# Two layers of a hybrid diffusion block: the reordered boundary of the layers, and five weight tiles of layer 1 abreast

## The reference

```python
for l in range(DEPTH):                                   # DEPTH = 2
    mod_l = split(silu(c) @ ada_w[l] + ada_b[l], 6)      # shift, scale, gate for two sub-layers
    mod_c = split(silu(c_ctx) @ ada_w[l] + ada_b[l], 6)
    hl = rmsnorm(xl, norm_mix_pre[l]) * (1 + mod_l[1]) + mod_l[0]
    hc = rmsnorm(xc, norm_mix_pre[l]) * (1 + mod_c[1]) + mod_c[0]
    zl, zc = hl @ w_in[l], hc @ w_in[l]                  # 24 tiles of 128 columns
    ... four branches of token mixing on z (attention, scan), gates from h, output projection w_o
    xl = xl + mod_l[2] * rmsnorm(m_l, norm_mix_post[l])
    f_l = conv_ffn(modulate(rmsnorm(xl, norm_ffn_pre[l]), mod_l[3], mod_l[4]), ...)   # ffn_up, ffn_down
    xl = xl + mod_l[5] * rmsnorm(f_l, norm_ffn_post[l])
    # the context stream goes through the same in layer 0 only
```

## Time and profile before

| | us |
|---|---|
| median of 3 runs | 1652.36 (1651.51 to 1654.15) |
| profiled execution | 1652.26 |
| its span | 1650.2 |
| TensorE busy (matmuls) | 1586.6 (96%) |
| VectorE busy | 944.0 (57%) |
| ScalarE busy | 799.6 (48%) |
| GpSimd busy | 312.5 (19%) |

### The profile page before, as it was taken

How to read it: one execution, slowest core, us unless ns; L and a number is a source line. 1 busy time by engine, 2 the same in 40 slices (tenths; PEclk the granted TensorE clock), 3 DMA queues, 4 the chain that set the end, 5 groups by cost and what they waited for, 6 DMA issues and landing times.

```text
span 1650.2 us, 33271 instructions
## 1 busy us (share of the span) xinstructions
PE 1586.6 (96%) x14140; PEld 1321.7 (80%) x14140; DVE 944.0 (57%) x1497; ACT 799.6 (48%) x1315; POOL 312.5 (19%) x251
## 2 busy tenths in 40 slices
PE   8999999988899999999999999999998889999998
PEld 6788767767678887888888886987877779899987
DVE  5364555565465569655554225655776277677764
ACT  4322456473354266443443225525766365566653
POOL 0160234323110000112222000312352220012210
PEclk9999999999999999999999999999999899999999
DMA  9753334223852352322226343843413285645453
GB/s 332 198 166 102 102 103 160 75 99 102 266 192 91 113 191 77 102 91 88 95 71 111 106 123 126 261 128 115 143 56 130 55 281 179 215 165 181 164 189 134
DMA packets 213889, 234.42 MB, mean 142 GB/s; under 512 B 5936, under 2 KB 194736, under 8 KB 213744
## 3 DMA queue, kind: packets, MB, share of 16 engines
q1 hardware_dynamic: 194208, 191.14, 35.3%
q0 software_dynamic: 14928, 34.87, 7.9%
q10 hardware_dynamic: 4608, 6.29, 1.1%
HBM read 216.55 MB, written 15.73 MB: 141 GB/s over the span
## 4 chain that ended last, share of the span: by engine, by line
PE 70%; DVE 4%; issue 3%; ACT 3%; DMA 0%; POOL 0%; ACTq 0%; DVEq 0%; POOLq 0%
PE ps L2337 15%; PE ps L2338 15%; PE ps L2339 15%; PE ps L2633 1%; PE ps L2645 1%; PE ps L2428 1%; PE ps L2794 1%; PE ps L2793 1%; PE ps L2792 1%; PE ps L2685 1%; PE ps L2402 1%; PE ps L2404 1%; PE ps L2403 1%; PE ps L2362 1%; PE ps L2363 1%
## 5 line engine op out<-in xcount | busy, mean ns | idle before, releaser
L1065 ACT ACTIVATE whi<-ring 128x1024 fp32r<-128x1024 f32 (+1 forms) x262 | 274.5, 1052 | 481.6 <-PE ps L2339 424.6
L1610 DVE TENSOR_TENSOR wlo<-ring,whi 128x1024 fp32r<-128x1024 f32 (+1 forms) x262 | 327.5, 1254 | 175.5 <-ACT whi L1065 174.8
L2337 PE MATMUL ps<-H,whi 128*128 128x256 f32 (+1 forms) x640 | 215.4, 337 | 1.8 <-DVE wlo L1610 1.8
L2339 PE MATMUL ps<-H,wlo 128*128 128x256 f32 (+1 forms) x640 | 214.9, 336 | 0.0
L2338 PE MATMUL ps<-H,whi 128*128 128x256 f32 (+1 forms) x640 | 214.9, 336 | 0.0
L2337 PE MATMUL ps<-HR,whi 128*128 128x512 f32 (+1 forms) x568 | 202.1, 356 | 0.5 <-DVE wlo L1610 0.3
L2339 PE MATMUL ps<-HR,wlo 128*128 128x512 f32 (+1 forms) x568 | 198.3, 349 | 0.0
L2338 PE MATMUL ps<-HR,whi 128*128 128x512 f32 (+1 forms) x568 | 198.2, 349 | 0.0
L2337 PEld LDWEIGHTS ps<-H,whi 128*128 128x128 f32 x640 | 122.3, 191 | 14.2 <-issue 1.9
L2338 PEld LDWEIGHTS ps<-H,whi 128*128 128x128 f32 x640 | 122.2, 191 | 12.2
L2339 PEld LDWEIGHTS ps<-H,wlo 128*128 128x128 f32 x640 | 122.3, 191 | 12.0
(11 more groups left out here) (397 smaller groups left out, 3279.9 us busy)
## 6 DMA issues: line engine op xcount, KB each, us to landing
ring<-in_ffn_up SPq DMA_DIRECT2D x44, 1024.0 KB, 5.0
ring<-in_w_gate SPq DMA_DIRECT2D x32, 1024.0 KB, 5.9
ring<-in_ada_w SPq DMA_DIRECT2D x32, 1024.0 KB, 5.3
ring<-in_w_in SPq DMA_DIRECT2D x24, 1024.0 KB, 7.6
ring<-in_ffn_down SPq DMA_DIRECT2D x10, 1024.0 KB, 5.0
ring<-in_ffn_down SPq DMA_DIRECT2D x18, 512.0 KB, 3.8
ada<-in_ada_w SPq DMA_DIRECT2D x8, 1024.0 KB, 11.7
WB<-in_w_branch POOLq DMA_DIRECT2D x8, 1024.0 KB, 6.5
```

Source lines behind the costliest of these rows:

```text
L1065: act.activation(whi[HALF_SLOT[m]][:, 0:kn, :], ring_half(raw, half, kn), ACT.Copy).then_inc(hi_done, 1)
L1610: dve.tensor_tensor(wlo[HALF_SLOT[m]][:, 0:kn, :], ring_half(raw, half, kn), whi[HALF_SLOT[m]][:, 0:kn, :].bitcast(F32), ALU.subtract).the ...
L2337: pe.matmul(o[:, c0:c1], hi[:, i, :], part(0, k), start=(k == 0), stop=False)
L2339: last = pe.matmul(o[:, c0:c1], lo[:, i, :], part(0, k), start=False, stop=(k == kn - 1))
```

## The change

Five things change, and all lie in layer 1:

1. `project_first` gets the first five tiles of z. Steps 0 to 2 (`SECOND_STEPS` = 3) are done for three tiles, then steps 0 to 2 for the other two, then steps 3 and 4 for all five, then the last three steps tile by tile. It waits for a tile's halves only when it comes to it, so the dummies, nine now, no longer wait for them. Tiles 3 and 4 use `whi` 3 and 4.
2. ScalarE and VectorE split the five tiles in pieces between the steps of the norm: the first before the root, the second behind it, the third after h 0, the other two after step 3 (ScalarE) or 4 (VectorE).
3. In `norm_finish` the high half of h 0 stands right behind its modulation, ahead of that of h 1, and in `norm_apply` its low half right behind the scaling of h 1. Both hold in the middle of layer 1 too.
4. VectorE's four small vectors (`omu`, `oka`, `hka`, `hwa`) go from ahead of the norm to behind it.
5. One modulation job of the second gap in the middle of layer 1 goes: every job from number 2 of layer 1's row moves one place ahead, and the new place is step 10 of attention. The middle then has two dummies in place of three, and one gap buffer load less.

```diff
-IDLE = {"z": 11, "up": 3}
+IDLE = {"z": 9, "up": (3, 2)}
+SECOND, SECOND_STEPS = 5, 3
...
-    after = [("gap", 1, 0), ("att", 1, 4)] + chunks(1) + [("gap", 1, 1)] * 2 + [("gap", 1, 2)] * 2
+    after = [("gap", 1, 0), ("att", 1, 4), ("att", 1, 10)] + chunks(1) + [("gap", 1, 1)] * 2 + [("gap", 1, 2)]
...
+    z = HALF[blocks_of(("z", 1, Z_ORDER[0]))[0]]
+    extra.update({z + n: n for n in range(SPLIT, SECOND)})
...
+                for i in range(KT):
+                    modulated(i)
+                    if i != 1:
+                        high(max(0, i - 1))
+                    if i in splits:
+                        split_until(splits[i])
+                high(KT - 1)
...
-                    split_until(half_no(("z", l, Z_ORDER[0])) + SPLIT)
+                    first_z = half_no(("z", l, Z_ORDER[0]))
+                    split_until(first_z + 1)
                     norm_root(l, 0)
+                    split_until(first_z + 2)
                     fill(("gap", l, 0))
-                    norm_finish(l, 0, Z, HR)
+                    norm_finish(l, 0, Z, HR, {0: first_z + SPLIT, SECOND_STEPS: first_z + SECOND})
...
                 for i in range(KT):
                     over_rms(l, k, src, tmp, i)
-                    if i >= 2:
-                        low(i - 2)
+                    if i != 2 and i:
+                        low(max(0, i - 2))
+                    if splits and i in splits:
+                        split_until(splits[i])
...
+                    split_until(first_z + 1)
+                    norm_apply(l, 0, X, Z, HR, {0: first_z + 2, 1: first_z + SPLIT, SECOND_STEPS + 1: first_z + SECOND})
...
-                tiles = []
-                for name in names:
-                    tiles += halves(name)
                 for _ in range(idle):
                     pe.matmul(outs[0][:, 0:256], K("ones"), con[:, 0:256], start=True, stop=True)
-                order = [(k, n) for k in range(ABREAST) for n in range(len(names))]
+                early = SECOND_STEPS if ahead else 0
+                order = [(k, n) for k in range(early) for n in range(ahead)]
+                order += [(k, n) for k in range(early) for n in range(ahead, len(names))]
+                order += [(k, n) for k in range(early, ABREAST) for n in range(len(names))]
                 order += [(k, n) for n in range(len(names)) for k in range(ABREAST, KT)]
                 for k, n in order:
+                    if n == len(tiles):
+                        tiles += halves(names[n])
```

50 lines of the change are left out of this document (23 added, 27 removed).

## The result

The changed kernel takes 1659.74 us (median of 14 runs, 1650.54 to 1665.10) where the kernel before took 1652.71 beside it (14 runs, 1648.17 to 1659.70): ratio 1.0046, 95% interval 1.0030 to 1.0062, slower by 7.0 us between the medians. Two more comparisons of the same kernel gave 1.0057 (1.0037 to 1.0077) and 1.0038 (1.0017 to 1.0060). The forecast was 1651.2, no change; its range ended at 1654.3. Four of the 142 executions of before that ran beside the experiments were in a slow state (1671 us and more) and are left out of all ratios. The profiled execution took 1661.82 us with a span of 1658.9 (before: 1650.2) and a mean granted clock of 0.986 (0.990). TensorE's share of the chain that ended last is again 70%; the page doesn't show the loss.

What follows compares the result with a forecast made beforehand. It took TensorE to bound the kernel, 70% of the chain, with time won only where it waits or does dummy work. Boundary -0.1, middle -1.3, attention +0.35 took 1652.26 to 1651.2 us; range 1648.0 to 1654.3.

Steps and rivals of the forecast that it cites:

- Boundary, forecast -0.1: Start of layer 1: 1.4 us gained at full clock, less 1.3 for a clock fall behind the wait for h 1.
- each of the two waits: TensorE at the boundary: forecast 0.75 us for the third tile's low half and 2.3 us for h 1.
- Rival A: Boundary: the wait for h 1 leaves the clock alone, so the 1.4 us gain stays; 1649.9 us, chance 0.18.
- Attention, forecast +0.35: Layer 1's attention: moved job adds 1.00 + 0.53 us on TensorE, mostly swallowed by later waits; bounds 0 and 1.55.
- Middle, forecast -1.3: Middle of layer 1: one modulation product, its transposition and a dummy leave, h 0 comes earlier; bounds 0.6 and 1.6.
- The sum: Whole kernel: 1652.26 - 0.1 - 1.3 + 0.35 = 1651.2 us, from boundary, middle and attention.
- a wait of 0.7 for h 1: Middle of layer 1: the new order brings h 1 only at 1450.2, so TensorE waits 0.7 us behind the first step.
- From there TensorE is full until it waits 1.12 ... These swallow most: End of layer 1's attention: waits of 1.12 us for GpSimd's pr and 0.78 for prT absorb most of the job.
- Rival D: Scan stages: shifted banks and ring turns add or spare waits; 1652.26 - 1 ± 3 us, chance 0.12.
- Rival C: Job paid in full in attention, first scan stage 1.55 late, full clock falls; 1654.5 us, chance 0.11.
- three of the four waits of 2.3 us or more: Profile before: four such waits between products; the clock stayed at 1.00 behind one and fell behind three, hence 1.3 taken.

Runs made afterwards that it cites:

- h3_place: Changed kernel with the moved modulation job in step 6 of layer 1's attention, not step 10; ratio 1.0032 to the kernel before.
- boundary alone: The change without the moved modulation job, with the middle's three dummies and loads as before; ratio 1.0001 to the kernel before.
- h2_hold: Changed kernel with SyncE's fourth gate load of layer 1 held until the first w_branch tile has landed; ratio 1.0025 to the kernel before.
- h1_pad: Kernel before with its eleven dummies split up, same columns, ten more instructions ahead of layer 1's work; ratio 1.0020 to the kernel before.
- h5_back: Changed kernel with four dummies of 512 columns for nine of 256; ratio 1.0004 to the kernel before.
- k3_four: Changed kernel with four dummies of 256 columns in place of nine; ratio 1.0002 to the kernel before.
- before again: One more profiled execution of the unchanged kernel before, to test whether one profile is enough; 1648.13 us.
- k1_after: The changed kernel again, without edits, beside control runs on the same chip; ratio 1.0038 to the kernel before.
- h6_bonus: Changed kernel with GpSimd's two products on bm in layer 1 held until VectorE has made both halves of TN; ratio 1.0027 to the kernel before.
- e2_job: Kernel before with the moved modulation job alone, its loads, and two dummies in the middle of layer 1; ratio 1.0027 to the kernel before.
- k2_ahead: Changed kernel with eighteen dummies of 128 columns for nine of 256; ratio 1.0023 to the kernel before.
- m2_fourholds: Changed kernel with four dummies of 256 columns, GpSimd's bm products behind TN and the fourth gate load behind the first w_branch tile; ratio 1.0012 to before.
- its twin: Changed kernel with four dummies of 512 columns, GpSimd's bm products behind TN and the fourth gate load behind the first w_branch tile; ratio 0.9984 to before.

## Why the prediction was wrong

**Boundary, forecast -0.1: right beside the profile it was made from.** Measured 0.0 in the three traces of the table, and -0.2 to 0.5 in the fifteen with the new order. The places come out within 0.3 us and each of the two waits 0.3 shorter; the clock falls behind them, in all fifteen, and z 0 ends as before (1049.49 less 2.1 is 1047.4). The Trainium skill's rule that I weighed, gaps below about 3 us ("TensorE: Matmul & The Clock Gate", section "Why this matters for your kernels"), would have kept 1.4; the 0.54 above speaks against it once more. Rival A is out. What I did not see: the first trace of before has a fall at its boundary, and so has one other of the five with the old boundary; the other three have none and are 0.4 us shorter. Against those the new order loses 0.4.

**Attention, forecast +0.35: right.** 0.27 to 0.35 in thirteen traces with the job in the tenth step; the wait for pr swallowed it as worked out.

**Middle, forecast -1.3: the size was off.** From ScalarE's root (rt from ps and eps) to its second rt of the feed-forward part (from ps and vec), before took 32.63 with a fall of the clock and 31.13 without; the changed kernel 31.65 with, and 30.17 without (`h3_place`). Like against like that is 0.98 and 0.96. The job alone took 31.32 with a fall, the boundary alone 31.66 without: so the new order of halves costs 0.3 to 0.5. The sum had it as a net gain: h 0 earlier, against a wait of 0.7 for h 1. The waits came out at 0.17 and 0.34, but real products started only 0.25 us ahead of those of the job alone (1448.58 for 1448.83), which waited once, for 0.36, and not for h 1. And the fall is not evenly spread: six traces with the job still in the middle have it twice, thirteen with both the job gone and the new order twelve times. Those thirteen average 31.54, the four with the middle as it was 31.52: over many executions nothing is left of the gain that the traces could show.

**The step that failed** is the sentence "From there TensorE is full until it waits 1.12 ... These swallow most", with what stands behind it: that a job hidden in attention leaves the rest of the layer as it was. The sum has no term for the recurrence; the three traces of the changed kernel show 6.3 to 6.8 us at its end. The job cost the attention only its 0.3, but two things changed for the recurrence.

First, ten more instructions (eight in all, with two dummies fewer) stand in front of it. In four of the six traces that have this count, `h2_hold` among them, a stall of 1.3 to 1.5 us then stands right before w_branch may be issued. `h1_pad` brings such a stall with instructions alone, and `h5_back` and `k3_four`, with five instructions fewer, are without it and without the loss in the median. From there the traces show a chain: issue in a tie with a gate load, landing 3.5 us slower, a wait of 3.55 to 3.94 for WL, two falls of the clock, 6.3 to 6.8 us together. That this chain is all of the 7 us of the medians is argued, not shown (see below the table).

Second, the wait for pr is gone, and TensorE and VectorE stand otherwise against GpSimd, on the shared port: a wait of 1.84 us for TN in eight traces, which costs little by itself. The clock's fall went from the products ahead of it to those behind it, in five of those eight, and the start grew by 2.5 to 3.0 us in the changed kernel, where before again has 0.9. That the wait causes the fall is not shown: `k1_after` and `h6_bonus` have such a fall behind a wait of 0.61.

Rival D had the place, the scan stages, but another mechanism (banks and ring turns); it gave 3 us either way a chance of 0.12 and nothing to tell it by. Rival C forecast that the job is paid in attention, which it is not. The loss is at D's place at twice D's price. The range was drawn from single falls of the clock; it left out that one stall delays a load and the load makes the next wait. The rows held a hint: three of the four waits of 2.3 us or more on which I judged the clock are stalls, two of them in the recurrences of layer 0 and one in that of layer 1, and I did not ask what a change of place would do to them.

**Open.** What the stall waits for isn't shown. In all six traces with it (three of the changed kernel, `e2_job`, `h1_pad`, `h2_hold`) one load of instructions (0.02 MB) starts 8.4 to 9.3 us behind the first gate load, while the DMA engines are full (share 1.08 from 1336 to 1338, after); but it starts in the same range in four traces without it as well. The Trainium skill, "Runtime: NRT & Kernel Launch", section "Instruction fetch mechanics", says that instructions come by DMA in blocks of 256, ahead of use and mostly hidden; that fits the stall's moving with a handful of instructions (two more in the program, five or six records earlier), but it would hide them, and here 1.5 us aren't. Nor is it shown why `h6_bonus` and `h3_place` have no stall, where `k2_ahead` loses its 0.23%, or why `m2_fourholds` is slower than its twin.

## What to carry to other kernels

Work hidden in a full stage is free only for that stage: ask which engine arrives earlier or later at the next one, and whom it meets there. Where a load may be issued only behind the last product of a stage, look at what else is queued for DMA at that moment; in three traces 1.7 us of lead lost went with 3.5 us more of landing and, with the clock's falls, some 6 us of time; holding the other load back won 1.5 us of the landing. When a change of place alone moves the time by half a per cent, vary the number of dummy instructions before you judge it: four for nine undid the loss in the median here. And take more than one trace of the kernel before: where the first one happens to have a fall of the clock, a change that only moves it looks like a gain.

## What the runs showed of the hardware

- The same program, before, takes 1644.7 to 1664.3 us (138 executions). Between its two traces the rest of layer 1's recurrence differs by 4.8 us, the 83 us of large products behind it by 0.01; over all twenty traces that stretch moves by 0.03.
- Whether the clock falls behind a wait of 1.8 us differs between executions of like stretches: behind TN's 1.84 it fell in five of eight traces.
- A dependent loop can stay at the low clock for 18.8 us (`h3_place`); its steps take 4.48 us there for 2.53.
- One VectorE product with both operands in SBUF took 1.93 for 0.69 us beside two GpSimd products of 1.41 together; before, it kept its 0.69 and a GpSimd product took 1.27 for 0.72. VectorE's products of the same size that read PSUM kept 0.68 in all traces.
- Ten more instructions with no more work cost 0.20% (0.05 to 0.35), at this one place in this kernel.
- Every trace has eleven to eighteen waits of TensorE of over 0.6 us, up to 3.3 us long, for nothing that the profile shows, nearly all in the recurrences.
